# Projection of two branches as seven-product parts, with gating and merging on GpSimd

## The chip, the cores and the metric

One core of one Trainium2 chip. The metric is the device time in microseconds of one execution. TensorE does the matmuls, ScalarE and VectorE copy, split and add, GpSimd gates tiles and issues DMAs, SyncE (SP) issues the weight loads.

## What is computed

One layer of a decoder for 520 tokens (512 of a prompt, 8 samples), D_MODEL = 2048, all in float32. h = RMSNorm(x) goes through one input projection to two mixers: a gated MLP with spatial gating (result `o_a`, 1024 channels) and a sparse attention with three branches (`o_b`, 8 heads x 128 = 1024 channels). Then

```
mix = sigmoid(g_a) * (o_a @ w_proj_gmlp) + sigmoid(g_b) * (o_b @ w_proj_nsa)
x = x + mix @ w_out
hm = rmsnorm(x, g_mlp_norm)
return x + square(relu(hm @ w_up)) @ w_down
```

where g_a and g_b, 2048 channels each, are also columns of h's input projection. The change concerns the first of these lines.

## The kernel before

Everything is kept transposed: channels on partitions, the 520 tokens along the free axis, in two halves of HT = 260. A float32 matmul is made of three in fp32r: each operand is split into a high part (`_hi`, ScalarE's copy, which rounds) and a low part (`_lo`, VectorE's subtraction of the high part from the source), and hi x hi, hi x lo and lo x hi are added in PSUM. Each matmul has 128x128 weights and 260 columns.

**Units.** One output tile of 128 channels over 16 input tiles is a unit (`unit`, L916; matmul in L943): 4 chunks x 4 tiles x 3 x 2 halves = 96 matmuls. Weights come as halves of 512 KB into `w_raw` (four slots, SP's queue), are split in chunks of 128x512 by `hi` (L1510) and `lo` (L2069) and stand in the four slots of `w_hi` and `w_lo`.

**Pairs.** The last 14 of the 16 pairs of gate tiles are done as seven-product parts (a Strassen-Winograd scheme on 2x2 blocks): a `Pair` is 7 products of 24 matmuls, 168 instead of 192. `TIMES` is the order of the second factors: B11, B21, T2, T1, T3, B22, T4. VectorE makes four sums of weight blocks per pair (`st_sums`, L2611 to L2621); ScalarE and VectorE split each product's 128x1024 weights into a slot of a ring (`ring_in`, L1798 and L2602); ScalarE copies partial results out of PSUM (`st_copy`, L1809, `st_c21`, L1814), VectorE adds others from PSUM (`st_added`, L2630) and scales by rstd (`st_scale`, L2636), ScalarE takes the tanh (`st_tanh`, L1818), GpSimd makes it a sigmoid and stores the tile to DRAM in `merge_d` (`gate_half`, L3204 and L3207, a tiny `carry`, L608, ahead of it). The ring has four slots up to pair 12 and three in pair 13, the last (`RING_END`); slots 2 and 3 lie in parts of `a_hi` and `a_lo` that the second factors leave free. TensorE's `st_pair` (L1319) waits ahead of the products for the weights (`ff_lo`), for st_copy (`ff_copied`: 1, 2, 3, 4 ahead of products 2, 4, 5, 6, counted from 0) and for st_added (`ff_read`, ahead of product 3).

**Projection.** Inside pair 13 and behind it `mixed` (L1723, L2513) splits `u_t` (o_a) and `q_t` (o_b) into a_hi and a_lo. Then 16 units run, one per output tile, each with two groups of chunks: chunks 0 and 1 are o_a's product and go to one pair of PSUM banks, chunks 2 and 3 are o_b's. VectorE multiplies each by its gates from `g_in` (L2700, L2705), which GpSimd's queue loads from `merge_d` (L3239), adds the two (L2707), and ScalarE and VectorE split the sum into `b_hi` and `b_lo` (L1871, L2710), the operand of the 16 output units that follow (x2_sum, L2746; GpSimd spills and squares in `x2_spill`, L3269 to L3278). Then the MLP runs in further seven-product parts.

Each engine's order is written out by hand, so an instruction that waits holds all that stands behind it on its engine.

Of the kernel before, what the change touches and what calls it, by code (L numbers as in the profile page):

```python
# [30 lines left out]
F32 = mybir.dt.float32  # L31
# [18 lines left out]
CH = 4  # L50
# [15 lines left out]
U_OUT = U_PROJ + MB  # L66
# [65 lines left out]
def base_of(g, k):  # L132

    first = N_ST * U_COUNTS[k]
    return first if whole(g, 0) else BODY_TOTAL[k] * g + (first + FIRST_TOTAL[k] - BODY_TOTAL[k])


RING, RING_END = (0, 1, 2, 3, 0, 1, 2), (0, 1, 2, 0, 1, 2, 1)


class Pair:


    def __init__(self, n):
        self.n = n
# [13 lines left out]
class Part:  # L159
# [134 lines left out]
def build(nc, t):  # L294
    with ExitStack() as ctx:
# [176 lines left out]
        o4 = o3 + 16 * A_HALF  # L472
        y_mid = at("y_mid", [P, 4, 4 * HT], o4)
# [36 lines left out]
        act_src = sem("act_src")  # L510
# [72 lines left out]
        g_loaded = [sem(f"g_loaded{n}") for n in range(2)]  # L583
        x_in_loaded = [sem(f"x_in_loaded{n}") for n in range(2)]
# [78 lines left out]
        MIXED_EARLY = (0, 2, 4, 6)  # L663
        MIXED_ORDER = MIXED_EARLY + (1, 3, 5, 7) + tuple(range(GRP, KT))
# [6 lines left out]
        def st_ring(hi, n):  # L671
            if n < 2:
                return (w_hi if hi else w_lo)[:, 2 * n:2 * n + 2, :]
            return (a_hi if hi else a_lo)[:, KT // 2:KT:2, HT:HT + 2 * P] if n == 2 else (
                a_hi if hi else a_lo)[:, 0:KT // 2:2, HT:HT + 2 * P]

        def st_weights(hi, n, j):
            per = 4 if n < 2 else 2
            return st_ring(hi, n)[:, j // per, (j % per) * P:(j % per + 1) * P]

        def st_source(p, k):
            src = st_sum[:, :] if k in (2, 5) else w_raw[:, (0, 1, None, 2, 0, None, 3)[k], :]
            return src.rearrange("p (a b) -> p a b", a=2 if p.ring(k) < 2 else 4)
# [115 lines left out]
        def _(sp_):  # L799
# [32 lines left out]
            for m in range(N_ST):  # L832
                p = Pair(m)
                for n, (signal, count) in ((2, (ff_lo, p.e + 4)), (1, (ff_sum, p.sums + 4)), (0, (ff_lo, p.e + 5)),
                                           (3, (ff_lo, p.e + 7))):
                    sp_.wait_ge(signal, count)
                    if m < N_ST - 1:
                        sp_.dma_start(w_raw[:, n, :], t["w_st"][4 * m + 4 + n]).then_inc(ff_loaded[n], 16)
                    else:
                        load_half(U_PROJ // 2, n)  # L840
            load_units(U_PROJ // 2 + 1, UNITS // 2)
# [73 lines left out]
        def _(pe):  # L915
            def unit(u, ah, al, ready, need, hooks=(), before=None, projections=False,  # L916
                     first_hook=None, among=None):
# [5 lines left out]
                for c in range(CH):  # L923
                    pe.wait_ge(lo_split, 4 * n + c + 1)
                    pe.wait_ge(ready, need(c))
                    if projections:
                        v = c // 2
                        if c % 2 == 0:
                            pe.wait_ge(mm_read, 2 * n - U_PROJ - 1 + v)
                    else:  # L930
                        v = u[1]
                        if c == 0 and type(n) is int and n < 4:
                            pe.wait_ge(first_read, n - 1)
                        elif c == 0:
                            pe.wait_ge(mm_read, before(u) if before else n - 1)
                    first = c % 2 == 0 if projections else c == 0
                    final = c % 2 == 1 if projections else c == CH - 1
# [382 lines left out]

            def st_pair(p):
                for b in range(NP):
                    pe.wait_ge(ff_lo, p.e + b + 1)
                    if b == 0 and p.n < 2 and st_odd(p):
# [11 lines left out]
                    st_product(p, b)  # L1336

            for n in range(N_ST):
                st_pair(Pair(n))

            def first_projection():
                pe.wait_ge(ff_c21, N_ST - 1)
                pe.wait_ge(ff_read, 3 * (N_ST - 1))

            unit((U_PROJ // 2, 0), a_hi, a_lo, a_ready, lambda c: KT + (6, 8, 12, 16)[c], projections=True,
                 first_hook=first_projection)
            unit((U_PROJ // 2, 1), a_hi, a_lo, a_ready, lambda c: KT + CK * (c + 1), projections=True)
            with pe.Fori(1, MB // 2) as i:
                for p in range(2):
                    unit((U_PROJ // 2 + i, p), a_hi, a_lo, a_ready, lambda c: KT + CK * (c + 1),  # L1350
                         projections=True)
            late = lambda u: num(u) + MB - 1
            with pe.Fori(0, MB // 2) as i:
                for p in range(2):
                    unit((U_OUT // 2 + i, p), b_hi, b_lo, b_ready, x_need, before=late)
# [2091 lines left out]
```

## Time and profile before

| | before |
|---|---|
| median of 3 runs | 2602.4 us (2601.48 to 2602.43) |
| span of the profiled execution | 2600.4 us; its own time is not among those shown, the median is 2.0 above the span |
| TensorE matmuls | 2588.5 us busy, 21487 instructions |
| VectorE, ScalarE, GpSimd | 1953.5, 1405.3, 458.6 us busy |
| projection, first to last matmul | 928.47 to 1113.20 us |

How to read it: the page gives busy times over the whole span and in 40 slices. The views behind it give groups of instructions, instructions in order of time, and busy time per stretch. An idle engine costs nothing unless TensorE waits for what it does next.

### The profile page before, as it was taken

The numbers are of one execution on the slowest core, as the hardware profiler recorded it, in microseconds if no ns is written. First come the engines' busy times: TensorE is split into PE (matmuls) and PEld (weight loads), VectorE is DVE, ScalarE is ACT, GpSimd is POOL, SyncE is SP. The second block draws the span as 40 slices with busy tenths as digits, with TensorE's granted clock in tenths as the row PEclk, the third lists the DMA queues.
The fourth block names the chain that finished last, engine by engine and source line by source line (L and its number), as shares of the span: only waits on it lengthen the run. The fifth ranks groups of instructions, "written<-read, shape, count | busy, mean of one in ns | idle before, by whom it ended". The sixth has DMA issues, their size and how long they took to land. (4 is left out here: it accounts for less than half of the span.)

```text
span 2600.4 us, 57446 instructions
## 1 busy us (share of the span) xinstructions
PE 2588.5 (100%) x21487; PEld 2560.1 (98%) x21487; DVE 1953.5 (75%) x2897; ACT 1405.3 (54%) x2415; POOL 458.6 (18%) x629
## 2 busy tenths in 40 slices
PE   9999999999999999999999999999999999999998
PEld 8999999999999999999999999999999999999998
DVE  6456646668777764455688888888888888898888
ACT  6445436556454442222366666666566665666656
POOL 2001350001121110023202121121121211112113
PEclk9999999999999999999999999999999999999999
DMA  6633552214344344434336575665766756657568
GB/s 212 203 114 114 164 173 74 66 50 132 125 142 137 123 163 138 132 128 145 118 114 159 149 182 144 169 158 149 174 149 167 169 144 166 156 160 175 140 169 180
DMA packets 125325, 378.79 MB, mean 146 GB/s; under 512 B 14258, under 2 KB 15922, under 8 KB 124944
## 3 DMA queue, kind: packets, MB, share of 16 engines
q1 hardware_dynamic: 69328, 245.36, 28.3%
q0 software_dynamic: 52704, 126.25, 22.5%
q10 hardware_dynamic: 3168, 5.45, 0.6%
q8 instruction: 87, 1.43, 0.2%
q14 instruction: 38, 0.31, 0.0%
HBM read 292.29 MB, written 91.00 MB: 147 GB/s over the span
## 5 line engine op out<-in xcount | busy, mean ns | idle before, releaser
L2762 DVE TENSOR_TENSOR w_lo<-w_raw,w_hi 128x1024 fp32r<-128x1024 f32 x351 | 428.0, 1222 | 105.9 <-ACT w_hi L1892 104.5
L1892 ACT ACTIVATE w_hi<-w_raw 128x1024 fp32r<-128x1024 f32 x352 | 370.9, 1062 | 203.0 <-PE aux L1365 69.8
L2069 DVE TENSOR_TENSOR w_lo<-w_raw,w_hi 128x512 fp32r<-128x512 f32 x280 | 202.3, 724 | 340.3 <-ACT w_hi L1510 339.7
L1365 PE MATMUL aux<-at_t,w_hi 128*128 128x260 f32 x2304 | 416.7, 282 | 0.2
L1510 ACT ACTIVATE w_hi<-w_raw 128x512 fp32r<-128x512 f32 x280 | 175.3, 628 | 411.5 <-PE mm L943 391.2
L943 PE MATMUL mm<-a_hi,w_hi 128*128 128x260 f32 x1728 | 357.5, 288 | 0.0
L1365 PEld LDWEIGHTS aux<-at_t,w_hi 128*128 128x128 f32 x2304 | 354.9, 188 | 0.7 <-DVE w_lo L2762 0.3
L1429 PE MATMUL aux<-fb_mid,w_hi 128*128 128x260 f32 x1920 | 352.1, 283 | 1.4 <-DVE w_lo L2762 1.1
L943 PE MATMUL mm<-a_hi,w_lo 128*128 128x260 f32 x1728 | 347.9, 283 | 0.0
L943 PE MATMUL mm<-a_lo,w_hi 128*128 128x260 f32 x1728 | 347.2, 282 | 0.0
L1365 PE MATMUL aux<-at_t,w_lo 128*128 128x260 f32 x1152 | 325.4, 282 | 0.0
L1429 PEld LDWEIGHTS aux<-fb_mid,w_hi 128*128 128x128 f32 x1920 | 295.8, 188 | 2.9 <-DVE w_lo L2762 1.3
L943 PEld LDWEIGHTS mm<-a_hi,w_hi 128*128 128x128 f32 x1728 | 266.7, 188 | 5.8 <-issue 4.4
L1429 PE MATMUL aux<-fb_mid,w_lo 128*128 128x260 f32 x960 | 271.2, 282 | 0.0
L943 PEld LDWEIGHTS mm<-a_hi,w_lo 128*128 128x128 f32 x1728 | 266.1, 188 | 0.0
L943 PEld LDWEIGHTS mm<-a_lo,w_hi 128*128 128x128 f32 x1728 | 266.0, 188 | 0.0
L1429 PE MATMUL mm<-fb_mid,w_hi 128*128 128x260 f32 x1440 | 265.1, 283 | 0.0
L1365 PE MATMUL mm<-at_t,w_hi 128*128 128x260 f32 x1280 | 232.5, 282 | 0.0
L1429 PEld LDWEIGHTS mm<-fb_mid,w_hi 128*128 128x128 f32 x1440 | 222.3, 188 | 0.0
L1365 PEld LDWEIGHTS aux<-at_t,w_lo 128*128 128x128 f32 x1152 | 216.8, 188 | 0.0
L3302 POOL TENSOR_TENSOR cell<-cell 128x1 f32<-128x1 f32 x62 | 20.7, 334 | 1060.0 <-ACT y_mid L1945 1048.1
L1429 PE MATMUL mm<-fb_mid,w_lo 128*128 128x260 f32 x720 | 203.8, 283 | 0.0
(483 smaller groups left out, 5827.9 us busy)
## 6 DMA issues: line engine op xcount, KB each, us to landing
w_raw<-in_w_ff SPq DMA_DIRECT2D x256, 512.0 KB, 3.5
w_raw<-in_w SPq DMA_DIRECT2D x142, 512.0 KB, 3.5
out_y_t<-y_mid POOLq DMA_DIRECT2D x120, 520.0 KB, 8.0
w_raw<-in_w_st SPq DMA_DIRECT2D x56, 512.0 KB, 3.6
g_in<-merge_d POOLq DMA_DIRECT2D x16, 520.0 KB, 4.9
merge_d<-z POOLq DMA_DIRECT2D x18, 260.0 KB, 4.0
st_f<-in_x_p POOLq DMA_DIRECT2D x8, 520.0 KB, 4.5
pages<-in_cache_cmp POOLq DMA_DIRECT2D x16, 256.0 KB, 4.1
```

Of the source, the lines that this page charges most:

```text
L943: last = pe.matmul(mm[:, 2 * v + h, 0:HT], w, a[:, kt, h * HT:(h + 1) * HT], start=first and k == 0 and part == 0, stop=final and k == CK ...
L1365: last = pe.matmul(dst, w, at_t[:, j, e:e + HT], start=FRESH[b] and j == 0 and part == 0, stop=j == KP - 1 and part == 2, skip_group_check ...
L1429: last = pe.matmul(dst, w, fb[:, j, e:e + HT], start=FRESH[b] and j == 0 and part == 0, stop=j == 1 and part == 2, skip_group_check=not FR ...
L1510: run(w_hi[:, c, :], raw(u, c), ACT.Copy).then_inc(hi_split, 1)
L1892: run(hi_of(p, k), source(p, k), ACT.Copy).then_inc(ff_hi, 1)
L2069: dve.tensor_tensor(w_lo[:, c, :], raw(u, c), w_hi[:, c, :].bitcast(F32), ALU.subtract).then_inc(lo_split, 1)
L2762: dve.tensor_tensor(lo_of(p, k), source(p, k), hi_of(p, k).bitcast(F32), ALU.subtract).then_inc(ff_lo, 1)
L3302: pool.tensor_tensor(cell[:, 2:3], cell[:, 0:1], cell[:, 1:2], ALU.mult).then_inc(cell_step, 1)
```

## The change

The projection becomes 8 more pairs, 14 to 21 (`N_PAIRS` = 22; `p.part` 0 to 7; pair 13 is part -1): four for o_a (phase 0), then four for o_b (phase 1). One covers 4 output tiles over 8 input tiles, in 7 products of 2 x 4 x 3 = 24 matmuls; its results are twice as wide (a copy or an add is of 2 x 260), in two PSUM banks each. The ring has three slots from pair 13 on, with a place `LATE` for one of them in pairs 20 and 21. The weights come in the layout of the gate pairs, four blocks of 512 KB per pair.

The second factors are quadrants of u_t and q_t (128 x 4 x 260 = 1040 elements) and their differences. GpSimd makes the differences (T1 of both in pair 7, the others from pair 13 on) and two low parts of o_a's (T1, B22); ScalarE and VectorE split the rest, `gm_hi` and `gm_lo` in pairs 13 and 14, `nsa_hi` and `nsa_lo` in 15 to 17 (in 15 and 16 in halves of 520).

A pair's result stays in SBUF (`mix_a` for phase 0, `b_f` for phase 1). GpSimd multiplies it by the gates, 128x1040 at a time, two per pair, and in phase 1 adds phase 0's result, two more (`gated`); for the second half of pair 21 VectorE does both. ScalarE and VectorE split the sum (`b_hi_in`, `b_lo_in`) one pair later, from pair 19 on. The gates are loaded as 8 tiles of 128 x 4 x 520. The output operand, and with it the MLP's operands at_t, x_home, fb_end and y_end, move to other places in SBUF. Behind pair 21 the first output unit needs two of the eight split halves for each of its chunks.

```diff
-U_OUT = U_PROJ + MB
+N_PROJ = 8
+N_PAIRS = N_ST + N_PROJ
+U_OUT = U_PROJ
...
-        return (RING_END if self.n == N_ST - 1 else RING)[k]
+        if self.n < N_ST - 1:
+            return RING[k]
+        r = (NP * (self.n - N_ST + 1) + k) % 3
+        return LATE if r == 2 and self.part >= N_PROJ - 2 else r
...
+            if p.part >= 0:
+                return (mm if st_odd(p) else aux)[:, 2 * k:2 * k + 2, 0:HT]
             return (mm if st_odd(p) else aux)[:, k, 0:HT]
 
         def st_out(p, t_):
+            if p.part >= 0:
+                return mix_a[p.q][:, t_:4:2, :] if p.phase == 0 else b_f[:, 4 * p.q + t_:4 * p.q + 4:2, :]
...
+            def mix_operand(p, j, b, part):
+                k = TIMES[b]
+                if p.phase:
+                    return nsa_part(part, k)[:, j, :]
+                first, half = GM_PLACE[k]
+                return (a_hi, a_lo)[part][:, first + 2 * j, BOTH[half]]
+
+            def mix_product(p, b):
+
+                dst = st_bank(p, 1 if b in (1, 3, 5) else 0)
+                fresh = b in (0, 1, 3)
+                for m in range(2):
+                    for j in range(4):
+                        wh, wl = (st_weights(hi, p.ring(b), 4 * m + j) for hi in (True, False))
+                        for w, part, k in ((wh, 0, 0), (wh, 1, 1), (wl, 0, 2)):
+                            last = pe.matmul(dst[:, m, :], w, mix_operand(p, j, b, part),
+                                             start=fresh and j == 0 and k == 0, stop=j == 3 and k == 2,
+                                             skip_group_check=not fresh)
+                last.then_inc(ff_used, 1)
...
+                    if p.part >= 0:
+                        mix_ready(p, b)
+                    if b == 0 and p.part in (0, 1):
...
+            def gm_hi(k):
+
+                if k in (T2, T4):
+                    act.wait_ge(mix_src, {T2: GM_T2, T4: GM_T4}[k])
+                elif k in (T1, T3):
+                    act.wait_ge(mix_src, {T1: GM_T1, T3: GM_T3}[k])
+                else:
+                    act.wait_ge(u_mixed, NH)
+                    act.wait_ge(aux3_read, 4 * NH)
+                act.wait_ge(ff_used, Pair(N_ST - 1).used + {B11: 1, B21: 1, T2: 2, T1: 2, T3: 6, B22: 6, T4: 1}[k])
+                run(gm_part(a_hi, k), gm_source(k), ACT.Copy).then_inc(mix_hi, 1)
+
+            def nsa_hi(k, js=slice(0, 4)):
+
+                if k == T4:
+                    for t_ in range(2):
+                        act.wait_ge(g_stored[t_], 16 * MB)
+                act.wait_ge(mix_src, {T1: NSA_T1, T2: NSA_T2, T3: NSA_T3, T4: NSA_T4}.get(k, NSA_T1))
+                act.wait_ge(ff_used, Pair(N_ST - 1).used + NP)
+                run(nsa_part(0, k, js), nsa_source(k, js), ACT.Copy).then_inc(mix_hi, 1)
+
+            def b_hi_in(p, t_):
+
+                if p.part == N_PROJ - 1 and t_ == 1:
+                    act.wait_ge(end_mixed, 1)
+                else:
+                    act.wait_ge(b_mixed, 2 * p.q + t_ + 1)
+                run(mixed_part(b_hi, p, t_), mixed_part(b_f, p, t_), ACT.Copy).then_inc(b_split, 1)
...
+                if p.part == -1:
+                    gm_hi(B11)
+                    gm_hi(B21)
+                if old and old.part < 0:
                     st_tanh(old, 0)
-                if end:
-                    act.wait_ge(u_mixed, NH)
-                    act.wait_ge(aux3_read, 4 * NH)
-                    mixed_tiles(0, 4)
+                if p.part == 0:
+                    gm_hi(T3)
+                    gm_hi(B22)
+                if p.part in (1, 2):
+                    nsa_hi(B11, slice(2 * p.part - 2, 2 * p.part))
+                    nsa_hi(B21, slice(2 * p.part - 2, 2 * p.part))
+                if p.part == 3:
+                    nsa_hi(T2)
+                if p.part > 4:
+                    b_hi_in(old, 0)
                 st_copy(p, 1)
                 ring_in(p, 5)
-                if old:
+                if old and old.part < 0:
                     st_tanh(old, 1)
+                if p.part == -1:
+                    gm_hi(T2)
+                if p.part == 0:
+                    gm_hi(T4)
+                if p.part in (1, 2):
+                    nsa_hi(B22, slice(2 * p.part - 2, 2 * p.part))
+                    nsa_hi(T1, slice(2 * p.part - 2, 2 * p.part))
+                if p.part == 3:
+                    nsa_hi(T3)
                 st_copy(p, 2)
                 ring_in(p, 6)
+                if p.part == -1:
+                    gm_hi(T1)
+                if p.part == 3:
+                    nsa_hi(T4)
+                if p.part > 4:
+                    b_hi_in(old, 1)
...
+            def gm_lo(k):
+
+                dve.wait_ge(mix_hi, GM_HI[k])
+                if k == T2:
+                    dve.wait_ge(mix_src, GM_T3)
+                dve.tensor_tensor(gm_part(a_lo, k), gm_source(k), gm_part(a_hi, k).bitcast(F32), ALU.subtract
+                                  ).then_inc(mix_lo, 1)
...
+                gate = old and old.part < 0
+                js = slice(2 * p.part - 2, 2 * p.part)
                 if old:
                     st_sums(p, 1)
                     st_sums(p, 2)
                     ring_in(p, 2)
-                    st_scale(old, 0)
+                    if gate:
+                        st_scale(old, 0)
                     ring_in(p, 3)
                 st_sums(p, 3)
                 if old:
                     st_added(p, 0)
                 ring_in(p, 4)
-                if old:
+                if p.part == -1:
+                    gm_lo(B11)
+                    gm_lo(B21)
+                if p.part == 0:
+                    gm_lo(T3)
+                if p.part in (1, 2):
+                    nsa_lo(KP + 4 * p.part + 4, B11, js)
+                    nsa_lo(KP + 4 * p.part + 5, B21, js)
+                if p.part == 3:
+                    nsa_lo(KP + NP + 9, T2)
+                if p.part > 4:
+                    b_lo_in(old, 0)
+                if gate:
                     st_scale(old, 1)
-                else:
+                elif not old:
                     tile_out(N_SMP + N_HOST)
-                if end:
-                    mixed(0, 4)
                 ring_in(p, 5)
+                if p.part == 0:
+                    gm_lo(T4)
+                if p.part in (1, 2):
+                    nsa_lo(KP + 4 * p.part + 6, B22, js)
+                if p.part == 3:
+                    nsa_lo(KP + NP + 10, T3)
                 ring_in(p, 6)
+                if p.part in (1, 2):
+                    nsa_lo(KP + 4 * p.part + 7, T1, js)
+                if p.part == 3:
+                    nsa_lo(KP + NP + 11, T4)
+                if p.part > 4:
+                    b_lo_in(old, 1)
...
+            def subtracted(dst, x, y, count):
+                pool.tensor_tensor(dst, x, y, ALU.subtract).then_inc(mix_src, 1)
+                pool.wait_ge(mix_src, count)
...
+            def load_gates(p):
+                for t_ in range(2):
+                    pool.wait_ge(g_stored[t_], 64 * (p.q + 1))
+                pool.dma_start(g_in[p.part % 2][:, :, :], merge_d.rearrange("(q k t) p n -> t q p k n", k=4, t=2)[
+                    p.phase][p.q]).then_inc(g_loaded[p.part % 2], 16)
+
+            def low(k):
+                pool.wait_ge(mix_hi, GM_HI[k])
+                pool.tensor_tensor(gm_part(a_lo, k), gm_source(k), gm_part(a_hi, k).bitcast(F32), ALU.subtract
+                                   ).then_inc(mix_lo_pool, 1)
+
+            end = Pair(N_ST - 1)
+            pool.wait_ge(ff_used, end.used + 2)
+            subtracted(gm_part(a_f, T2), quadrant(u_t, B22), quadrant(u_t, T1), GM_T2)
+            subtracted(gm_part(a_f, T4), quadrant(u_t, B21), gm_part(a_f, T2), GM_T4)
+            pool.wait_ge(mix_lo, GM_LO[B21])
+            subtracted(quadrant(u_t, T3), gm_part(a_f, T2), quadrant(u_t, B11), GM_T3)
+            low(T1)
             pool.wait_ge(v_stored, 16)
+            pool.wait_ge(ff_used, end.used + NP)
+            load_gates(Pair(N_ST))
+            low(B22)
             for p in range(2):
-                pool.wait_ge(g_stored[p], 16 * (MB - 1))
-            pool.wait_ge(ff_used, Pair(N_ST - 1).used + 5)
-            for p in range(2):
-                load_gates(0, p)
-            for p in range(2):
-                gate_half(MB - 1, p, st_out(Pair(N_ST - 1), p))
-            for p in range(2):
-                pool.wait_ge(g_stored[p], 16 * MB)
-            with pool.Fori(1, MB // 2) as i:
-                for p in range(2):
-
-                    pool.wait_ge(mm_read, U_PROJ + 2 * (2 * i + p) - 2)
-                    load_gates(i, p)
-            pool.wait_ge(mm_read, U_OUT + MB)
-            pool.wait_ge(b_ready, MB)
+                gate_half(MB - 1, p, st_out(end, p))
+            subtracted(nsa_source(T2), quadrant(q_t, B22), quadrant(q_t, T1), NSA_T2)
+            subtracted(nsa_source(T3), nsa_source(T2), quadrant(q_t, B11), NSA_T3)
+            pool.wait_ge(st_made, 2 * N_ST)
+            subtracted(nsa_source(T4), quadrant(q_t, B21), nsa_source(T2), NSA_T4)
+            pool.wait_ge(mix_lo, GM_DONE)
+            pool.wait_ge(mix_lo_pool, GM_DONE_POOL)
+            load_gates(Pair(N_ST + 1))
+
+            def gated(p, t_):
+                if t_ == 0:
+                    pool.wait_ge(g_loaded[p.part % 2], 16 * (p.part // 2 + 1))
+                    pool.wait_ge(ff_read, p.read + 3)
+                else:
+                    pool.wait_ge(ff_c21, p.c21 + 1)
+                y = st_out(p, t_)
+                carry(nc.gpsimd)
+                steps.did(pool.tensor_tensor(y, y, gate_part(p, t_), ALU.mult))
+                if p.phase:
+                    pool.tensor_tensor(y, y, mix_a[p.q][:, t_:4:2, :], ALU.add).then_inc(b_mixed, 1)
+
+            for i in range(N_PROJ):
+                p = Pair(N_ST + i)
+                for t_ in range(2 if i < N_PROJ - 1 else 1):
+                    gated(p, t_)
+                if i + 2 < N_PROJ:
+                    load_gates(Pair(N_ST + i + 2))
+            pool.wait_ge(b_ready, N_PROJ)
```

## Rows read from the trace of the kernel before

**Rows 1.** The page: span and busy times of TensorE and its weight loads

```profile
span 2600.4 us, 57446 instructions
PE 2588.5 (100%) x21487; PEld 2560.1 (98%) x21487; DVE 1953.5 (75%) x2897; ACT 1405.3 (54%) x2415; POOL 458.6 (18%) x629
```

**Rows 2.** Busy time by stretch (gate pairs; pair 13; projection), order of columns first

```profile
core 0: us, PE busy (x) PEld busy (x) DVE busy (x) ACT busy (x) POOL busy (x), PEclk, DMA share, GB/s
645.50:908.20 262.70, 262.70 (x2194) 262.63 (x2194) 202.83 (x209) 128.33 (x181) 48.35 (x75) 1.00 0.39 130
908.20:928.40 20.20, 20.20 (x170) 20.04 (x168) 17.06 (x22) 13.21 (x22) 6.23 (x8) 1.00 0.41 129
928.40:1113.20 184.80, 184.78 (x1538) 184.70 (x1537) 90.35 (x138) 54.30 (x91) 13.28 (x20) 1.00 0.44 143
```

**Rows 3.** TensorE by time: first matmuls of pair 13, projection, output units

```profile
908.18 0.28 PE L1317 MATMUL aux<-a_hi,w_hi 128*128 128x260 f32 x1
...
928.47 0.48 PE L943 MATMUL mm<-a_hi,w_hi 128*128 128x260 f32 x2
...
1113.20 0.40 PE L943 MATMUL mm<-b_hi,w_hi 128*128 128x260 f32 x2
```

**Rows 4.** ScalarE by time: the copy behind the end of two successive pairs

```profile
888.25 0.39 ACT L1814 ACTIVATE z<-aux 128x260 f32<-128x260 f32 x1 [1.76 <-PE aux L1317]
...
908.38 0.39 ACT L1814 ACTIVATE z_odd<-mm 128x260 f32<-128x260 f32 x1 [1.48 <-PE mm L1317]
```

**Rows 5.** ScalarE by time in pair 13: the second tanh

```profile
919.02 0.62 ACT L1818 ACTIVATE z_odd<-z_odd 128x520 f32<-128x520 f32 x1
```

**Rows 6.** GpSimd by time: in pair 12 and in pair 13

```profile
894.03 0.88 POOL L608 TENSOR_TENSOR small<-ones 128x1 f32<-128x1 f32 x1 [13.17 <-ACT z L1818]
...
920.01 1.60 POOL L3204 TENSOR_SCALAR z_odd<-z_odd 128x520 f32<-128x520 f32 x1
921.91 0.58 POOL L3207 DMA_DIRECT2D merge_d<-z_odd  x1 [0.30 <-POOL z_odd L3204]
```

**Rows 7.** VectorE by time in pair 13

```profile
910.42 1.22 DVE L2602 TENSOR_TENSOR a_lo<-st_sum,a_hi 128x1024 fp32r<-128x1024 f32 x1
...
919.91 1.22 DVE L2602 TENSOR_TENSOR a_lo<-st_sum,a_hi 128x1024 fp32r<-128x1024 f32 x1
923.89 1.23 DVE L2602 TENSOR_TENSOR w_lo<-w_raw,w_hi 128x1024 fp32r<-128x1024 f32 x1 [2.77 <-ACT w_hi L1798]
```

**Rows 8.** GpSimd by form (busy us, mean ns); the small one by time

```profile
L3153 POOL TENSOR_TENSOR acc_v<-acc_v,sq 128x520 f32<-128x520 f32 x8 | 10.4, 1305 | 0.6
...
1128.29 0.20 POOL L608 TENSOR_TENSOR small<-ones 128x1 f32<-128x1 f32 x1
```

**Rows 9.** VectorE and GpSimd by time, first output units

```profile
1125.60 0.69 DVE L2069 TENSOR_TENSOR w_lo<-w_raw,w_hi 128x512 fp32r<-128x512 f32 x1 [2.15 <-ACT w_hi L1510]
1128.53 1.52 DVE L2069 TENSOR_TENSOR w_lo<-w_raw,w_hi 128x512 fp32r<-128x512 f32 x1 [1.63 <-ACT w_hi L1510]
...
1128.43 1.06 POOL L3277 TENSOR_TENSOR x_sq<-x_home 128x520 f32<-128x520 f32 x1
1129.57 1.64 POOL L3278 TENSOR_TENSOR acc_x<-acc_x,x_sq 128x520 f32<-128x520 f32 x1
```

**Rows 10.** VectorE reading PSUM beside GpSimd, by time

```profile
393.50 0.69 DVE L2459 CUSTOM_DVE_ANT_0 p_long<-aux,toep 128x512 f32<-128x512 f32 x1
...
393.51 1.05 POOL L3152 TENSOR_TENSOR sq<-v_t 128x520 f32<-128x520 f32 x1 [11.92 <-ACT v_t L1654]
```

**Rows 11.** VectorE by form: scaling, adds from PSUM of 260 and of 520

```profile
L2636 DVE TENSOR_TENSOR z<-z,rstd 128x520 f32<-128x520 f32 x14 | 9.6, 691 | 0.0
L2630 DVE TENSOR_TENSOR z<-z,aux 128x260 f32<-128x260 f32 x14 | 5.8, 418 | 0.0
L2746 DVE TENSOR_TENSOR x_home<-mm,x_home 128x520 f32 x12 | 8.3, 693 | 0.0
```

**Rows 12.** DMA issues of the gate loads: KB each, median us to landing

```profile
g_in<-merge_d POOLq DMA_DIRECT2D x16, 520.0 KB, 4.9
```

More of the change, by code:

```diff
@@ L1335, in st_pair @@
                         pe.wait_ge(ff_read, p.read + 1)
-                    st_product(p, b)
-            for n in range(N_ST):
+                    (mix_product if p.part >= 0 else st_product)(p, b)
+            for n in range(N_PAIRS):
                 st_pair(Pair(n))
[L1341 to L1348, printed above, removed]
-                for p in range(2):
-                    unit((U_PROJ // 2 + i, p), a_hi, a_lo, a_ready, lambda c: KT + CK * (c + 1),
-                         projections=True)
-            late = lambda u: num(u) + MB - 1
+            pe.wait_ge(ff_c21, Pair(N_PAIRS - 2).c21 + 1)
+            pe.wait_ge(ff_read, Pair(N_PAIRS - 2).read + 3)
             with pe.Fori(0, MB // 2) as i:
                 for p in range(2):
-                    unit((U_OUT // 2 + i, p), b_hi, b_lo, b_ready, x_need, before=late)
+                    unit((U_OUT // 2 + i, p), b_hi, b_lo, b_ready, lambda c: 2 * (c + 1))
             def product(p, b, js=range(KP)):
@@ L1823, in _, with first_free @@
             ring_in(p, 1, (chunk_done, CH * U_PROJ))
+            def first_free(p, k):
+                return (b_ready, 2) if p.ring(k) == LATE and p.last_free(k) is None else None
             def st_pair(p):
                 old = Pair(p.n - 1) if p.n else None
-                end = p.n == N_ST - 1
                 if old:
@@ L1848, in st_pair @@
                 st_copy(p, 3)
-                if not end:
+                if p.part < N_PROJ - 1:
+                    to = Pair(p.n + 1)
                     for k in range(2):
-                        ring_in(Pair(p.n + 1), k)
-            for n in range(N_ST):
+                        ring_in(to, k, first_free(to, k))
+            for n in range(N_PAIRS):
                 st_pair(Pair(n))
-            p, u = Pair(N_ST - 1), (U_PROJ // 2, 0)
-            act.wait_ge(ff_used, p.used + 4)
+            p, u = Pair(N_PAIRS - 1), (U_OUT // 2, 0)
@@ L2676, in st_pair @@
                     st_sums(Pair(p.n + 1), 0)
+                else:
+                    lo((U_OUT // 2, 0), 0)
+                    lo((U_OUT // 2, 0), 1)
                 st_added(p, 2)
-                if not end:
+                if p.part == -1:
+                    gm_lo(T2)
+                if p.part < N_PROJ - 1:
                     ring_in(Pair(p.n + 1), 1)
-            for n in range(N_ST):
+            for n in range(N_PAIRS):
                 st_pair(Pair(n))
-            p = Pair(N_ST - 1)
@@ new lines, in _ @@
+            p = Pair(N_PAIRS - 1)
+            for c in range(2, CH):
+                lo((U_OUT // 2, 0), c)
+            dve.wait_ge(ff_c21, p.c21 + 1)
+            dve.wait_ge(ff_read, p.read + 2)
+            dve.wait_ge(g_loaded[p.part % 2], 16 * (p.part // 2 + 1))
+            steps.did(dve.tensor_tensor(st_out(p, 1), st_out(p, 1), gate_part(p, 1), ALU.mult))
+            dve.wait_ge(b_mixed, N_PROJ - 2)
+            dve.tensor_tensor(st_out(p, 1), st_out(p, 1), mix_a[p.q][:, 1:4:2, :], ALU.add).then_inc(end_mixed, 1)
```

254 lines of the change are left out of this document (135 added, 119 removed).

## The prediction, made before the change was run

> **What bounds the kernel now.** I read the page's busy shares first: TensorE is busy for 2588.5 of 2600.4 us and its weight loads for 98%, so only fewer matmuls, or idle time put between them, can move the end [rows 1]. Then the windows by stage. In the gate stage, the last gate pair and the projection TensorE has no idle time, and its granted clock is 1.00, which is the 2.4 GHz level [rows 2]. VectorE is the second engine: 202.83 of 262.70 us in the gate stage, but only 90.35 of 184.80 in the projection. Then TensorE's timeline at the borders, to time the stage exactly [rows 3], ScalarE's copies of one pair and the next for the length of a pair [rows 4], and last the three helpers inside the last gate pair, since their queues decide what the new work delays [rows 5 to 7].
>
> **Removed.** The projection runs from 928.47 to 1113.20: 184.73 us for 16 output tiles x 96 = 1536 matmuls [rows 3]. The new one is 8 pairs of 7 x 24 = 168 matmuls, 1344 in all. One pair of 168 takes 908.38 - 888.25 = 20.13 us [rows 4], so 8 take 161.0. Gain: **23.7 us**, if TensorE is never made to wait. Everything else is about that.
>
> **Pair 13, a wait moved into ScalarE's queue.** gm_hi(T2) now stands behind tanh(old, 1) and ahead of st_copy(13, 2), and it waits for a GpSimd subtraction which stands behind gate_half(12, 1). In the trace this tanh starts at 919.02 [rows 5] and GpSimd's last DMA issue for that gate half ends at 921.91 + 0.58 = 922.49 [rows 6]. The tanh comes some 0.4 later and the gate half's 1.60 us shrinks a little, so I keep 922.5. The subtraction is two-input, 128x1040. The trace has none of that size. A two-input one of 520 takes 1.305, a 128x1 can take 0.20 [rows 8], so 2.13 ns an element: 0.20 + 2.21 = **2.41 us**. Bounds: twice 1.06, the square that reads one tensor [rows 9], is 2.1; twice 1.305 is 2.6. I take the value between, since the change's operations read two tensors and the fixed part is paid once. So 924.9; gm_hi(T2) 0.95 more; st_copy(2) 0.4 more: 926.4. TensorE's sixth product needs that copy and should start at 908.18 + 5 x 2.876 = 922.56. Stall **4.0** (3 to 5). The Trainium skill's "GPSIMD Engine Reference" (§ 3, the measured numbers) gives 4497 ns for 2048 elements; as an estimate that is 2.28 for 1040, and my final number would be 3.2 us lower by it.
>
> **The sum that decides: VectorE and GpSimd don't run side by side.** While GpSimd ran its 1.06 us product at 1128.43, VectorE's 128x512 subtraction, 0.69 elsewhere, took 1.52: from 1128.53 it ended at 1130.05, which is GpSimd's end plus 0.56. GpSimd's next, at 1129.57, then took 1.64 instead of 1.3: it waited in turn [rows 9]. Inside dense VectorE work it is the same: the gate half's 0.62 took 1.60 behind a running subtraction [rows 6, 7]. So each waits for the instruction in flight, and they alternate. A VectorE operation with an input in PSUM isn't held: 0.69 at 393.50 beside GpSimd's 1.05 at 393.51 [rows 10]. The Trainium skill's "SBUF — State Buffer" (the shared port pair) calls it an exclusive lock for the whole instruction, for VectorE operations with two SBUF inputs against GpSimd ones that read SBUF; it speaks against this change, and these rows agree.
>
> So the two engines' times are added. VectorE per pair: 202.83 / (262.70 / 20.13) = 15.5 us [rows 2]. Without two scalings (0.69 each) and with three adds of 520 for 260 (0.69 for 0.42) [rows 11] it is **14.9**. Extra:
> - pairs 14 to 18: two scalings 1.4, low halves of T2, T3, T4 3.6 (T2's spills over from 13), two times four halves of 520 5.6, three of 1040 3.7: 14.3. VectorE: 5 x 14.9 + 14.3 = 88.8.
> - GpSimd there: two low halves, three subtractions for the second branch, and 2 gatings for each of 14 to 17: 13 x 2.41 = 31.3; two gate tiles 1.2; ten small ones 2.0: 34.5.
> - Sum 123.3 against 5 x 20.13 = 100.7: 22.6 over. Ten adds read PSUM, 6.9 us, and may lie under a GpSimd operation; I take half off: **19.2**.
> - pairs 19 to 21: VectorE 3 x (14.9 + 2.4) = 51.9; GpSimd gates and merges 18 to 20, 4 each: 12 x 2.41 + 1.2 = 30.1. 82.0 against 60.4; half of 4.1 off: **19.5**.
>
> VectorE's low half is ready about 2.3 us ahead of its product (911.64 for 913.93) [rows 7]; that head start is used up once: **-2.0**.
>
> **What I cost at nothing.** The two subtractions in pair 7: GpSimd waits 13.2 us there [rows 6], and VectorE has 4.6 idle; if it lacks them, 2. Three ring slots instead of four: pair 13 already runs on three without idle time. Gate loads: as many bytes, now 1040 KB two pairs ahead; the old ones landed in 4.9 [rows 12]; a late one would hold only GpSimd, for some 5 us. Weights: 4 x 512 KB a pair, as in the gate stage, on SP's queue behind the same signals. If VectorE is late they are requested late too, but all slots slip together. ScalarE: 13.21 of 20.2 [rows 2], and what it adds replaces mixed tiles. New waits on ScalarE: b_hi_in(old, 0) stands ahead of st_copy(p, 1), which product 4 needs 11.5 us into the pair; GpSimd's multiply and add of that half take 4.8 from about the pair's start, some 7 with VectorE between, so it is early; nsa_hi waits for GpSimd's three subtractions, which begin about 15 us before pair 17 at the latest. TensorE's new wait ahead of pair 18 for o_b's last low half: VectorE makes it before pair 17's last add. The output operand: chunks 0 to 2 of the first output tile (8.6 us) cover gating, merging and splitting of pair 21 on two engines, about 8; if that cover fails, 2. GpSimd's first x loads stand behind b_ready as before, and their sum is due only 20 us later. Later stages only change addresses.
>
> **Sum:** -23.7 + 4.0 + 19.2 + 19.5 - 2.0 = **+17.0**. The profiled span 2600.4 becomes 2617.4. The median shown is 2.0 above that span (and the three agree within 1 us); I carry the 2.0: **2619**.
>
> **Bounds of this case.** Low: 25 operations at 2.1 (-7.8) and all PSUM adds hidden (-5.5): +4. High: 2.6 (+4.8), none hidden (+5.5), and GpSimd's work bunched at the start of each pair, so that VectorE later idles behind ScalarE: +30. Own range 2607 to 2630.
>
> **Rivals.**
> 1. *Not slower: GpSimd's operations fall into VectorE's gaps.* Place: pairs 14 to 21. For it: VectorE idles 2.77 us at one place of pair 13 [rows 7], and the four gatings wait for nothing urgent. It decides where VectorE's and GpSimd's work in a pair is below 20.13 together; by my sum pair 18 alone is (14.9 + 5.0), 19 to 21 have 27. If the rows of the output stage don't hold for these tiles, only pair 13 and 1 us behind it are left: -23.7 + 5.0 = -18.7, **2584**. Chance 0.13.
> 2. *Partly:* the gate stage's 15.5 holds some waiting and the adds hide fully; the stalls come to 20 to 27: **2598 to 2606**. Chance 0.09.
> 3. *Worse: bunching.* GpSimd's four operations of pairs 19 to 21 all stand between the pair's start and its third product, whose low half then comes 12 us after the start instead of 3.5. Where VectorE can't make that up I add 4 a pair: **2630 to 2642**. Against it: they alternate, and half go ahead of need. Chance 0.12.
> 4. *The change doesn't do what it says:* the product count stands in the loops, so only a wait could cancel it. No chance of its own.
>
> Forecast case: 0.66. Within 0.2% (5.2 us, about what a measurement of this kernel can tell from no change) is 2597.2 to 2607.6: most of rival 2 and the forecast's edge, 0.08. Faster 0.13, slower 0.79. The range 2601 to 2636 holds nearly all of the forecast case, half of rival 2 and half of rival 3.
>
> **What would show it.** In the changed kernel's trace: TensorE's idle time no longer near 0 from 922 to the output tiles, ended mostly by VectorE's a_lo and w_lo; 1344 matmuls there; one gap of about 4 us ahead of pair 13's sixth product, ended by ScalarE's z copy behind a GpSimd subtraction; pairs 19 to 21 about 26 us long, pair 18 near 20; VectorE's 1.22 us subtractions at 2 to 3.6 us where GpSimd works, and its own alone near 2.4. It would be wrong if these VectorE operations keep 1.22, if pairs stay at 20.13, or if GpSimd's 1040 takes far from 2.4.

## The result, and the profile after

The change makes the kernel slower: 2631.5 us (2630.5 to 2632.8, four runs) against 2602.4; the ratio is 1.0113 with a 95% interval of 1.0099 to 1.0127. The profiled execution took 2632.8 us, its span is 2631.3. In the page, TensorE is busy a little less than in [rows 1], and for a smaller share of a longer span; GpSimd is recorded as busy for 113 us more, waits inside its operations included:

```profile
span 2631.3 us, 56723 instructions
PE 2585.1 (98%) x21295; PEld 2552.8 (97%) x21295; DVE 2066.6 (79%) x2891; ACT 1450.2 (55%) x2441; POOL 571.7 (22%) x668
```

21295 matmuls are 192 fewer, as the loops say. The stage ends later all the same: the first matmul of the output units is at 1145.5, where [rows 3] has 1113.20. The windows of the changed kernel, with the columns of [rows 2], from pair 13 to that matmul:

```profile
908.40:1145.30 236.90, 202.68 (x1524) 198.60 (x1524) 211.67 (x155) 110.87 (x139) 120.26 (x64) 0.92 0.36 123
...
908.40:932.30 23.90, 20.14 (x156) 19.96 (x156) 17.16 (x16) 12.73 (x18) 12.09 (x9) 0.93 0.31 104
932.30:960.00 27.70, 22.95 (x180) 21.76 (x180) 27.49 (x20) 14.32 (x18) 15.50 (x12) 1.00 0.35 123
960.00:985.00 25.00, 18.75 (x126) 18.16 (x126) 22.82 (x16) 9.39 (x13) 14.29 (x8) 0.86 0.47 166
...
1085.00:1110.00 25.00, 20.24 (x146) 19.71 (x145) 22.05 (x14) 9.36 (x12) 16.20 (x7) 0.86 0.28 82
```

Two things are to be seen in the first line. TensorE is idle for 236.9 - 202.7 = **34.2 us**, where it had no idle time. And its matmuls take longer. The window begins 1.4 us ahead of pair 13's first matmul (909.78), so pairs 13 to 21 take 235.7 us and TensorE is busy for 201.5 of them with 9 x 168 = 1512 matmuls, which at 20.13 us a pair [rows 4] need 181.2: **20.3 us** more. The mean granted clock of 0.92 accounts for at most 0.08 x 235.7 = 19 of them. The rest is lost at full clock, a little at each stop: the window from 932.30 has a clock of 1.00, and there 180 matmuls, which need 21.6 us, are recorded with 22.95.

The length of each pair, read as in [rows 4] from one copy of C21 to the next (here L1918), against 20.13:

| pair | 9 | 13 | 14 | 15 | 16 | 17 | 18 | 19 | 20 | 21 |
|---|---|---|---|---|---|---|---|---|---|---|
| changed kernel | 21.3 | 25.6 | 26.4 | 30.2 | 24.4 | 24.3 | 23.1 | 26.5 | 27.9 | 27.3 |

The excess is 5.5 in pair 13, 27.8 in 14 to 18, 21.2 in 19 to 21 and 1.2 in pair 9: 55.7. Less the 23.7 saved it is 32.0; the border is 32.3 later, since 0.4 us are lost ahead of the gate pairs. What TensorE waited for in all (us in total, times, longest), the eight longest after its start:

```profile
PE mm L1393 <- DVE w_lo L2738: 7.2, 5, 4.7
PE aux L1393 <- DVE a_lo L2738: 6.3, 2, 3.3
PE aux L1393 <- DVE w_lo L2738: 5.7, 2, 4.6
PE aux L1393 <- DVE mix_a L2766: 4.1, 2, 2.1
PE aux L1374 <- ACT z L1913: 3.8, 1, 3.8
...
PE mm L1393 <- DVE mix_a L2766: 2.5, 2, 2.1
PE mm L1393 <- DVE b_f L2766: 2.0, 1, 2.0
PE mm L1393 <- issue: 1.4, 1, 1.4
```

It is VectorE that is late, once ScalarE. Why, the order in time shows. VectorE in pair 19:

```profile
1065.05 1.22 DVE L2751 TENSOR_TENSOR st_sum<-w_raw 128x1024 f32<-128x1024 f32 x1
1066.19 3.46 DVE L2753 TENSOR_TENSOR w_raw<-w_raw 128x1024 f32<-128x1024 f32 x1
1069.57 3.40 DVE L2738 TENSOR_TENSOR a_lo<-st_sum,a_hi 128x1024 fp32r<-128x1024 f32 x1
1072.89 1.21 DVE L2738 TENSOR_TENSOR w_lo<-w_raw,w_hi 128x1024 fp32r<-128x1024 f32 x1
1074.03 3.43 DVE L2757 TENSOR_TENSOR st_sum<-w_raw,st_sum 128x1024 f32<-128x1024 f32 x1
```

GpSimd and TensorE over the same stretch:

```profile
1065.14 3.42 POOL L3431 TENSOR_TENSOR b_f<-b_f,g_in 128x1040 f32<-128x1040 f32 x1
1068.64 3.25 POOL L3433 TENSOR_TENSOR b_f<-b_f,mix_a 128x1040 f32<-128x1040 f32 x1
1071.85 1.17 POOL L627 TENSOR_TENSOR small<-ones 128x1 f32<-128x1 f32 x1
1072.98 3.39 POOL L3431 TENSOR_TENSOR b_f<-b_f,g_in 128x1040 f32<-128x1040 f32 x1
...
1073.03 0.80 PE L1393 MATMUL aux<-nsa_t,a_hi 128*128 128x260 f32 x2 [3.29 <-DVE a_lo L2738]
```

GpSimd's product waits for the sum that runs on VectorE (to 1066.27) and then takes 2.3; VectorE's next waits for it (to 1068.56) and takes 1.1; and so on in turn. A VectorE operation of 1.22 is recorded with 3.4. That low half is 3.3 us late for TensorE, and TensorE's next record is 0.80 for two matmuls where 0.40 was usual.

### The profile page after: what moved, and what is told of

It reads as the page before. It is cut to its first block and busy times, and to the rows that moved or that the text cites. A ratio compares the mean times of both kernels' runs of the same rounds, so it can differ in the third digit from the quotient of the medians.

```text
span 2631.3 us, 56723 instructions
## 1 busy us (share of the span) xinstructions
PE 2585.1 (98%) x21295; PEld 2552.8 (97%) x21295; DVE 2066.6 (79%) x2891; ACT 1450.2 (55%) x2441; POOL 571.7 (22%) x668
## 3 DMA queue, kind: packets, MB, share of 16 engines
q1 hardware_dynamic: 69328, 245.36, 27.8%
## 5 line engine op out<-in xcount | busy, mean ns | idle before, releaser
L1447 PE MATMUL aux<-at_t,w_hi 128*128 128x260 f32 x2016 | 368.2, 282 | 0.2 <-DVE w_lo L2906 0.2
L2190 DVE TENSOR_TENSOR w_lo<-w_raw,w_hi 128x512 fp32r<-128x512 f32 x216 | 158.3, 736 | 253.0 <-ACT w_hi L1592 252.3
L1447 PEld LDWEIGHTS aux<-at_t,w_hi 128*128 128x128 f32 x2016 | 310.4, 188 | 0.4 <-DVE w_lo L2906 0.4
L1447 PE MATMUL aux<-at_t,w_lo 128*128 128x260 f32 x1008 | 284.2, 282 | 0.0
L1000 PE MATMUL mm<-a_hi,w_hi 128*128 128x260 f32 x1216 | 254.4, 290 | 0.0
L1000 PE MATMUL mm<-a_hi,w_lo 128*128 128x260 f32 x1216 | 244.7, 283 | 0.0
L1000 PE MATMUL mm<-a_lo,w_hi 128*128 128x260 f32 x1216 | 244.2, 282 | 0.0
L1000 PEld LDWEIGHTS mm<-a_hi,w_hi 128*128 128x128 f32 x1216 | 187.8, 189 | 5.6 <-issue 3.8
L1000 PEld LDWEIGHTS mm<-a_lo,w_hi 128*128 128x128 f32 x1216 | 187.3, 188 | 0.0
L1000 PEld LDWEIGHTS mm<-a_hi,w_lo 128*128 128x128 f32 x1216 | 187.2, 188 | 0.0
```

The lines of the kernel that those rows point to most:

```text
L1000: last = pe.matmul(mm[:, 2 * v + h, 0:HT], w, a[:, kt, h * HT:(h + 1) * HT], start=first and k == 0 and part == 0, stop=final and k == CK ...
L1447: last = pe.matmul(dst, w, at_of(j)[:, e:e + HT], start=FRESH[b] and j == 0 and part == 0, stop=j == KP - 1 and part == 2, skip_group_chec ...
L2190: dve.tensor_tensor(w_lo[:, c, :], raw(u, c), w_hi[:, c, :].bitcast(F32), ALU.subtract).then_inc(lo_split, 1)
```

## The experiments

Theory A: GpSimd's operations that read SBUF and VectorE's with two inputs in SBUF don't run side by side. B: the new stage is too tight by itself. C: the results come too late because GpSimd is slow. Every run is compared with runs of the kernel before on the same chip: 2601.5 us for the first four (22 runs), 2601.8 for the last three (16 runs).

**1. The gating left out.**

```diff
-                steps.did(pool.tensor_tensor(y, y, gate_part(p, t_), ALU.mult))
-                if p.phase:
-                    pool.tensor_tensor(y, y, mix_a[p.q][:, t_:4:2, :], ALU.add).then_inc(b_mixed, 1)
+                n = 152 + 2 * (p.part % 4) + t_
+                steps.did(pool.tensor_tensor(small[:, 160:161], ones[:, 0:1], ones[:, 0:1], ALU.mult))
+                if p.phase:
+                    pool.tensor_tensor(small[:, n:n + 1], ones[:, 0:1], ones[:, 0:1], ALU.mult).then_inc(b_mixed, 1)
```

> Leaves out the gating products and the merging sums of pairs 14 to 21 that GpSimd did (22 operations of 128x1040 less one half pair's two, which VectorE keeps); a 128x1 operation with the same signals stands in for each. Theory A (GpSimd's SBUF reads hold VectorE): pairs 16 to 21, which took 4.2, 4.2, 3.0, 6.3, 7.8 and 7.1 us over 20.13, fall to 20.1 to 20.5, pair 15 loses some 3 of its 10; in all 2631.5 - 35 = about 2597 (2593 to 2601), VectorE's 1.22 us operations are 1.22 again there. Theory B (the stage is too tight by itself: three ring slots, ScalarE's new waits, wider adds): most of the excess stays, 2620 or more.

Measured: 2593.6 us, ratio 0.9968 (0.9955 to 0.9981). Pairs 16 to 21 are at 20.1 to 20.2, pair 15 at 24.6 instead of 30.2; pairs 9, 13 and 14 are as in the changed kernel (21.3, 25.6, 26.5). B falls for pairs 16 to 21: three ring slots, wider adds and ScalarE's new waits fit in 20.13 us there. Pairs 13 to 15 keep their other GpSimd work, so this run doesn't decide for them. C is not excluded by this, since the work is gone altogether.

**2. The same time on GpSimd, without reading.**

```diff
-                steps.did(pool.tensor_tensor(y, y, gate_part(p, t_), ALU.mult))
+                x = gate_part(p, t_)
+                def filled(d):
+                    steps.did(pool.memset(d, 0.5))
+                for _ in range(1 + p.phase):
+                    filled(x)
+                    filled(x)
+                    filled(x[:, 0, :])
...
-                    pool.tensor_tensor(y, y, mix_a[p.q][:, t_:4:2, :], ALU.add).then_inc(b_mixed, 1)
+                    n = 152 + 2 * (p.part % 4) + t_
+                    pool.tensor_tensor(small[:, n:n + 1], ones[:, 0:1], ones[:, 0:1], ALU.mult).then_inc(b_mixed, 1)
```

> As the changed kernel, but each of GpSimd's gating and merging operations is replaced by fills of constants that take about as long (near 2.5 us) and read nothing from SBUF; gating and merging are left out. Theory A in its narrow form (GpSimd's reads hold VectorE, writes don't): as with the gating left out, within 3 us, near 2598. Theory A in a wide form (any GpSimd access to SBUF holds): as the changed kernel, 2626 to 2636. Theory C (the results just come too late through GpSimd, whatever VectorE does): also 2626 to 2636, but then VectorE's operations keep 1.22 us.

Measured: 2597.0 us, ratio 0.998 (0.9969 to 0.999). Pairs 16 to 21: 20.6, 21.3, 20.9, 21.1, 20.1, 20.2. Pair 19 of this kernel, VectorE and GpSimd by time:

```profile
1051.85 1.22 DVE L2751 TENSOR_TENSOR st_sum<-w_raw 128x1024 f32<-128x1024 f32 x1
1052.98 1.22 DVE L2753 TENSOR_TENSOR w_raw<-w_raw 128x1024 f32<-128x1024 f32 x1
1054.19 1.23 DVE L2738 TENSOR_TENSOR a_lo<-st_sum,a_hi 128x1024 fp32r<-128x1024 f32 x1
1055.63 1.23 DVE L2738 TENSOR_TENSOR w_lo<-w_raw,w_hi 128x1024 fp32r<-128x1024 f32 x1 [0.21 <-ACT w_hi L1899]
...
1051.92 5.22 POOL L3433 MEMSET g_in<- 128x1040 f32 x6
```

GpSimd fills for 5.22 us without a break, and each of VectorE's operations keeps its 1.2. So GpSimd is at work for 5.2 us, longer than the 2 x 2.4 of the two operations by themselves (with the turns they took 6.75 in the changed kernel, from 1065.14 to 1071.89), and the stage keeps its speed: C falls, and A holds in its narrow form. It is the reading that holds. Most of the 3.4 us over experiment 1 is in pairs 16 to 19, where VectorE waited up to 2.8 us for ScalarE; ScalarE in turn waited 2.0 to 2.4 us there for a weight load, and why the loads were later wasn't followed.

**3. The wait in pair 13 put later.**

```diff
-                if p.part == -1:
-                    gm_hi(T2)
                 if p.part == 0:
                     gm_hi(T4)
...
                 ring_in(p, 6)
                 if p.part == -1:
+                    gm_hi(T2)
                     gm_hi(T1)
```

> Only the place of the copy that waits for GpSimd's T2 in pair 13 is changed: behind the copy out of PSUM and the split of product 6 instead of ahead of them. Theory A: the stall of 3.8 us ahead of the sixth product and the 1.6 us that pair 13 took more than it goes: 2626 to 2628. Rival: the slack is used up anyway, since VectorE has to catch up in pair 14: pair 14 grows by as much, 2630 to 2632.

Measured: 2630.4 us, ratio 1.0109 (1.0092 to 1.0125): 1.1 us less than the changed kernel, with the spreads of the two overlapping. Theory A's range is missed and the number lies in the rival's. The stall only halves, to 1.91. In the profiled executions pair 13 takes 23.8 instead of 25.6, and pairs 14 to 21 together 209.8 instead of 210.0: 14 and 17 are shorter (25.4 and 22.8 instead of 26.4 and 24.3), 16, 18 and 20 longer (25.0, 24.6 and 28.3 instead of 24.4, 23.1 and 27.9). So the rival's reason doesn't hold either: pair 14 doesn't grow, and what pair 13 gains stays. Behind pair 13 the time is as before, whatever becomes of the one wait.

**4. Gating and merging on VectorE.** `gated(old, 0)` stands behind ring_in(p, 3), `merged(old, 0)` behind st_added(p, 0), `gated(old, 1)` behind ring_in(p, 4), `merged(old, 1)` behind ring_in(p, 5). Of this work GpSimd keeps only the loads of the gates; the differences and the two low parts stay with it.

```diff
+            def gated(p, t_):
+                dve.wait_ge(g_loaded[p.part % 2], 16 * (p.part // 2 + 1))
...
+                dve.tensor_tensor(y, y, gate_part(p, t_), ALU.mult).then_inc(gated_made, 1)
+
+            def merged(p, t_):
...
+                dve.tensor_tensor(y, y, mix_a[p.q][:, t_:4:2, :], ALU.add).then_inc(
+                    end_mixed if (p.part, t_) == (N_PROJ - 1, 1) else b_mixed, 1)
```

> Gating and merging move from GpSimd to VectorE (1.14 us each instead of holding it for 2.4), one pair later as before; GpSimd keeps the quadrants' differences and two low parts. Theory A: pairs 19 to 21 carry 14.9 + 2.4 + 4.6 = 21.9 us of VectorE work, 1.8 over each, pairs 16 to 18 up to 1 over, pairs 13 to 15 keep some 20 over: 2602.4 - 23.7 + 26 = about 2605 (2598 to 2612). Theory B or C: VectorE, now with more work of its own, makes it slower: 2632 or more.

Measured: 2599.6 us, ratio 0.999 (0.998 to 0.9999). The profiled execution, from which the pairs are read, was the longest of ten (2602.4). Pairs 16 to 21: 20.5, 20.5, 20.6, 21.2, 21.9, 21.9; the sum of 21.9 is met in the last two. 32 us less than the changed kernel, by giving the busier engine 22 more operations. The estimate was 5 us too high.

**5. The kernel before with one hold**, to measure the slow matmuls by themselves. SyncE and GpSimd do what they did; one more DMA releases TensorE.

```diff
+                    if b == 5 and p.n in HELD:
+                        pe.wait_ge(held, 16 * (HELD.index(p.n) + 3))
...
+                if n in HELD:
+                    pool.wait_ge(ff_used, Pair(n).used + 5)
+                    pool.dma_start(held_d, rel_d).then_inc(held, 16)
```

> The kernel before, with one added hold: in gate pair 4 TensorE's sixth product waits for a small DMA (20 KB from DRAM to DRAM) that GpSimd issues once the fifth is done, some 3 us of idle time; nothing else changes. Theory K (a short stop also lowers TensorE's granted clock for a while, at 1.2 instead of 2.4 GHz, as the changed kernel's windows suggest): pair 4 grows by 1 to 2 us more than TensorE's idle time there, and a window of 25 us has a granted clock of 0.9 or so. Rival: the clock stays at 1.00 and the pair grows by the idle time alone, 3 us; the low clock of the changed kernel then has another reason (its work).

Measured: 2607.2 us, ratio 1.0022 (1.0011 to 1.0032), 5.4 us more than before for 3.34 us of idle time. Pair 4 takes 26.1. TensorE by time, and two windows:

```profile
744.95 0.56 PE L1320 MATMUL mm<-a_hi,w_hi 128*128 128x260 f32 x1 [3.34 <-DMA held_d<-rel_d]
745.30 0.42 PE L1320 MATMUL mm<-a_lo,w_hi 128*128 128x260 f32 x1
745.52 0.42 PE L1320 MATMUL mm<-a_hi,w_lo 128*128 128x260 f32 x1
745.73 0.42 PE L1320 MATMUL mm<-a_hi,w_hi 128*128 128x260 f32 x1
...
744.00:752.00 8.00, 7.05 (x39) 7.08 (x40) 2.22 (x4) 1.06 (x1) 0.00 (x0) 0.60 0.02 4
752.00:760.00 8.00, 8.00 (x69) 8.00 (x68) 7.33 (x8) 4.26 (x6) 0.80 (x1) 1.00 0.03 5
```

The matmuls behind the hold start 0.217 us apart (745.30 to 745.52 to 745.73) where 0.120 is usual: the 1.2 GHz level. The mean clock of that window is 0.60, and 1.00 in the next. The pair's 6.0 us are 3.3 idle and 2.7 in slower matmuls and the restart. Theory K holds; the expectation's 1 to 2 us was too low.

**6. Eight holds**, in pairs 2 to 9, `HELD = (2, ..., 9)`.

> The kernel before with that hold in each of the gate pairs 2 to 9, some 8 x 3 = 24 us of idle time. Theory K: 1 to 2 us more in each, together 34 to 40 us more than before. Rival: 24 us more. If the low clock comes only now and then, as in the changed kernel where some pairs lose no more than their idle time, something between, and uneven pairs.

Measured: 2642.3 us (two runs, 2639.8 and 2644.8), ratio 1.0157 (1.0139 to 1.0176): 40.5 more than before, with 27.5 us of idle time at the holds (read from the profiled run, 2639.8). The pairs grow by 5.1, 6.2, 5.1, 6.2, 5.2, 3.6, 4.0 and 3.7. Two windows of it:

```profile
783.00:808.00 25.00, 21.38 (x163) 21.19 (x163) 15.78 (x16) 9.84 (x14) 4.46 (x7) 0.91 0.32 107
...
833.00:858.00 25.00, 21.28 (x178) 21.10 (x177) 15.77 (x16) 9.84 (x14) 4.46 (x7) 1.00 0.31 108
```

The same hold, in the same place of the pair, costs 0.2 us beyond its idle time in the last three pairs, at full clock, and 1.6 to 3.0 in the first five. So idle time has a price besides itself, but not each time.

**7. All of GpSimd's work with two inputs that can move, on VectorE**: number 4, with number 3's order, and the two low parts, the second branch's three differences (in pair 15) and those of pair 7 (in pairs 8 and 9) on VectorE. GpSimd keeps T2, T4 and T3 of u_t.

```diff
+                if p.n == 8:
+                    subtracted(quadrant(u_t, T1), quadrant(u_t, T1), quadrant(u_t, B11), GM_T1)
+                if p.n == 9:
+                    subtracted(quadrant(q_t, T1), quadrant(q_t, T1), quadrant(q_t, B11), NSA_T1)
+                if p.part == 1:
+                    subtracted(nsa_source(T3), nsa_source(T2), quadrant(q_t, B11), NSA_T3)
```

> As with gating and merging on VectorE, and besides: the two low parts, the three differences of the second branch and those of pair 7 on VectorE too (1.14 us each instead of 2.4), and the copy of T2 in pair 13 behind product 6's split. Theory A: pair 14 comes from 26.5 to about 23, pair 15 from 25.7 to about 23, pairs 8 and 13 lose 1 each or more; in all 2599.6 - 8 = about 2592 (2588 to 2596), clear of the kernel before. Rival: VectorE is now the bound on its own in pairs 14 and 15 and the order of its queue costs what the moves gain: 2597 to 2601.

Measured: 2593.1 us (2591.7 to 2593.7), ratio 0.9966 (0.9954 to 0.9979): faster than the kernel before by 8.7 us and than the changed one by 38. Pairs 13 to 21: 22.2, 25.0, 22.0, 23.1, 20.5, 20.7, 20.5, 21.9, 21.9; pair 9 is at 20.1 again. The total is as theory A had it, but not each pair: 14 was to come to about 23 and takes 25.0, with VectorE busy for 24.0 of them (15 was to be about 23 too and takes 22.0). In pair 14 VectorE's own work is above a pair's 20.13, so there theory B is right in part. What TensorE waited for, its two longest:

```profile
PE mm L1394 <- DVE mix_a L2766: 2.9, 2, 1.6
PE aux L1375 <- ACT z L1914: 1.9, 1, 1.9
```

No stop is longer than 1.9 us, and from pair 13 to 1127 us the granted clock is 1.00.

## Why the prediction was right, and where its size fell short

Slower was forecast, with 0.79, by 17.0 us (2619); it is 29.1. The measured time is inside the range of 2601 to 2636, but just outside the forecast case's own 2607 to 2630 (the bounds +4 and +30 that it is drawn from would give 2606 to 2632), and inside the 2630 to 2642 of rival 3. Step by step:

- **The gain of 23.7** holds: with the gating left out pairs 16 to 21 take 20.1 to 20.2 (experiment 1).
- **Pair 13.** Right place and size: ScalarE's copy waited behind T2, and TensorE stood 3.76 us for it (4.0 forecast; the prediction's own terms add up to 926.3 and 3.7). GpSimd's T2 took 2.39 where 2.41 was worked out from rows of 520 and of 1:

```profile
924.15 2.39 POOL L3379 TENSOR_TENSOR a_f<-u_t 128x1040 f32<-128x1040 f32 x1
...
928.06 0.36 PE L1374 MATMUL aux<-a_hi 128*128 128x260 f32 x1 [3.76 <-ACT z L1913]
```

- **The sum of the two engines.** The mechanism is shown: by the turns that they take, and by experiments 1 and 2, which take away the work and then only its reading. The Trainium skill's "SBUF — State Buffer" (§ Who interferes with whom) says the same: a VectorE instruction with two SBUF inputs contends with a GpSimd one that reads SBUF, not with one that only writes it; experiments 1 and 2 agree (3.4 us against 1.22). The estimate of 2.28 us for 1040 elements from the Trainium skill's "GPSIMD Engine Reference" lies below the 2.39 measured. For idle time my terms gave 4.0 + 19.2 + 19.5 - 2.0 = 40.7; TensorE's idle time is 34.2.
- **The term that was mis-sized: time in which neither engine works.** Pairs 14 to 21 take 210.0 us; the forecast had 161.0 + 19.2 + 19.5 - 2.0 = 197.7. Two errors stand against each other in it. In the trace VectorE or GpSimd is at work for 192.2 us, where the forecast's added times, its halves taken off, come to 199.8. And for 17.8 us neither works, which the sum had at nothing; only its high bound names it ("VectorE later idles behind ScalarE"). That the total came out within 12.3 us is in part luck: 7.6 of the 17.8 were covered by prices that were too high. Two ways in which it comes about, in pairs 16 and 19, and the stop of pair 20:

```profile
1008.00 0.61 ACT L1913 ACTIVATE mix_a<-mm 128x520 f32<-128x520 f32 x1 [3.29 <-PE mm L1393]
1008.51 1.05 ACT L1899 ACTIVATE w_hi<-w_raw 128x1024 fp32r<-128x1024 f32 x1
1009.59 1.23 DVE L2738 TENSOR_TENSOR w_lo<-w_raw,w_hi 128x1024 fp32r<-128x1024 f32 x1 [2.31 <-ACT w_hi L1899]
...
1088.16 1.06 ACT L1899 ACTIVATE w_hi<-w_raw 128x1024 fp32r<-128x1024 f32 x1 [2.84 <-DMA w_raw<-in_w_st]
1089.25 1.23 DVE L2738 TENSOR_TENSOR w_lo<-w_raw,w_hi 128x1024 fp32r<-128x1024 f32 x1 [2.85 <-ACT w_hi L1899]
...
1101.43 0.59 PE L1393 MATMUL mm<-nsa_t,w_hi 128*128 128x260 f32 x1 [4.70 <-DVE w_lo L2738]
```

  In the first, TensorE has stopped for VectorE and then run at the low clock for a while; ScalarE's copy waits for TensorE's product, the split stands behind the copy, and VectorE waits for the split. In pair 18 it does so for 2.62 us with TensorE at full clock. In the second, a weight load comes late: VectorE, held by GpSimd, freed its slot late (the load is issued at 1080.83), and the load landed 7.3 us later. "All slots slip together" was wrong: while the load was on its way, VectorE had nothing to do.
- **The low clock, a second term that the forecast lacks.** "Its granted clock is 1.00" was read from a stage without idle time and carried into one with 34 us of it. That a stop can lower the clock is shown by experiment 5 in the unchanged kernel. But slower matmuls cost time only where TensorE isn't waiting for VectorE anyway, so their 20.3 us can't be added to the forecast's terms. In pair 13 the 1.7 us beyond the stop are of this kind (a clock of 0.93 over 23.9 us). Pairs 16 to 18 have one stop of 2.0 to 2.1 each; 16 and 17, with a part at the low clock, take 24.4 and 24.3, and 18, at 1.00, takes 23.1. Pair 15 of experiments 1 and 2 has the same stop (3.05 and 3.04) and takes 24.6 with a granted clock of 1.00 around it and 24.9 with 0.93. And of the changed kernel's four runs two had a mean clock of 0.992 and 0.993 (2632.8 and 2632.5 us) and two of 0.996 (2630.6 and 2630.5): some 0.0035 x 2630 = 9 us less in slow matmuls, and 2.1 us less time. So the clock is a part of the 15 us between 40.7 and 55.7, by these numbers the smaller one. An exact split isn't shown.
- **By pairs.** 14 to 18 took 27.8 over for 19.2, 19 to 21 21.2 for 19.5, pair 13 5.5 for 4.0, pair 9 1.2 for nothing. Pair 18 was to be near 20 and took 23.1, at full clock: VectorE is at work or held for only 18.5 of them, so it is the order of the waits that makes this pair long, not the sum.
- **Costed at nothing.** The subtractions of pair 7: pair 9 lost 1.2 (bound 2), and has it back in experiment 7. Ring, loads, the new waits of ScalarE other than pair 13's: nothing in pairs 16 to 21 as long as VectorE isn't held (experiment 1). In the changed kernel it is held, and there two late loads made ScalarE stand for 2.8 and 2.2 us. The output operand: the output stage takes 184.6 us with no stop, as before.
- **The rivals.** "Not slower" fell with the first record of 3.4 us. "Bunching" was true as a mechanism: in pairs 19, 20 and 21 the third product waited 3.3, 4.7 and 4.6 us for its low half, which came 9 to 11 us after the pair's start. The 4 us a pair that it was to add did not come on top: these pairs are 1.7 over the forecast's sum.
- Of the 32.3 us at the border 30.9 are left at the span's end and 29.1 in the medians. The MLP's instructions are the same; what gave 1 us back there wasn't followed.

## What to carry to other kernels

Before elementwise work goes to GpSimd to relieve VectorE, add the two engines' times: where both read SBUF and VectorE's operations have two inputs there, the sum has to fit, and 1.14 us of VectorE's time was bought here with 2.4 of both. Then look for what waits in a ring: an engine that is held frees its buffers late, its loads are asked for late, and it later stands idle for them, so that the sum is not the worst case. And a lone stall of TensorE in a stage where nothing else is late is to be priced above its length: the nine holds of experiments 5 and 6, each of some 3.4 us, cost 3.6 to 6.2 us. Where TensorE waits for another engine all along, the four runs of the changed kernel suggest that slower matmuls cost much less than their own length.

## What the runs showed of the hardware that was not expected

A single stop of 3.34 us was followed by matmuls 0.217 us apart instead of 0.120, and cost 2.7 us on top. Eight stops of 3.4 us in a row of equal pairs did it five times and three times not. The length of the stop alone doesn't decide it: in pair 13 a stop of 1.91 us (experiment 3) was followed by the low clock (0.89 from 920 to 935 us) and one of 1.88 (experiment 7) was not (1.00); in pair 15 one of 3.04 was (experiment 2) and one of 3.05 was not (experiment 1). What decides it, these runs don't show. And GpSimd's fills beside VectorE's subtractions slowed neither (5.22 us for four of 1040 and two of 520; 1.22 each), while one that reads a single column waited its turn (1.17 us for a 128x1 product).
